# Gathering the next expert's rows in two fp32r passes from a high and a low part

## What is computed

```python
logits = hf @ router_w                       # hf: 256 x 1024, 8 experts
top_vals, top_idx = lax.top_k(logits, 2)
top_w = jax.nn.softmax(top_vals, axis=-1)    # gates: 256 x 8, two entries of each row
for e in range(8):
    y = y + gates[:, e:e+1] * ((silu(hf @ wg[e]) * (hf @ wu[e])) @ wd[e])
```

## Time and profile before

| | |
|---|---|
| median of 3 runs | 1638.24 us (1637.22 to 1639.24) |
| profiled execution, its own time | 1640.91 us |
| its span, first to last instruction | 1639.2 us |
| mean granted TensorE clock | 0.967 |
| PE busy | 1547.0 us, 94% |
| PE weight loads busy | 1292.2 us, 79% |
| DVE busy | 1238.8 us, 76% |
| ScalarE busy | 915.4 us, 56% |
| GpSimd busy | 25.3 us, 2% |
| expert loop | from 814.3 us to about 1620 us |

### The profile page before, as it was taken

One profiled execution on the slowest core, in us unless ns is written; L12 is line 12 of the kernel. 1 busy time (PEld: TensorE's weight loads), 2 busy tenths in 40 slices (PEclk: granted clock), 3 DMA queues, 4 the chain that ended last, 5 costly groups with the idle time before them and its releaser, 6 DMA issues.

```text
span 1639.2 us, 23240 instructions
## 1 busy us (share of the span) xinstructions
PE 1547.0 (94%) x8684; PEld 1292.2 (79%) x8684; DVE 1238.8 (76%) x1408; ACT 915.4 (56%) x952; POOL 25.3 (2%) x60
## 2 busy tenths in 40 slices
PE   5899999899998999989599999999999999999996
PEld 4788777798997887777488888888888888888885
DVE  5969676474356587765688887988879888798886
ACT  5144553433233434543467776767777677676764
POOL 0000010000000000100000000000000000000000
PEclk9699999899899999999699999999999999999999
DMA  5253325444345253324288898988989889899893
GB/s 227 92 162 134 111 85 191 156 173 155 111 157 204 88 189 149 129 97 173 94 337 347 325 376 329 355 336 324 366 312 365 348 324 363 323 357 355 320 365 150
DMA packets 76638, 391.49 MB, mean 239 GB/s; under 512 B 28320, under 2 KB 28448, under 8 KB 29728
## 3 DMA queue, kind: packets, MB, share of 16 engines
q1 hardware_dynamic: 74960, 389.71, 63.2%
q10 hardware_dynamic: 1616, 0.92, 0.2%
HBM read 386.80 MB, written 1.05 MB: 237 GB/s over the span
## 4 chain that ended last, share of the span: by engine, by line
PE 86%; DVE 7%; ACT 4%; issue 2%; DMA 1%; POOL 0%; DVEq 0%; ACTq 0%; POOLq 0%; SPq 0%
PE psum L1609 25%; PE psum L1610 25%; PE psum L1611 25%; PE psum L1625 3%; PE psum L1666 2%; ACT w_hi L524 2%; DVE w_lo L530 2%; PE psum L1649 1%; PE psum L1876 1%; PE psum L1643 1%; DVE hsT_lo L1165 1%; PE psum L1668 1%; ACT prob L892 1%; PE psum L1708 1%; PE psum L1892 0%
## 5 line engine op out<-in xcount | busy, mean ns | idle before, releaser
L530 DVE TENSOR_TENSOR w_lo<-w_raw,w_hi 128x2048 fp32r<-128x2048 f32 x270 | 614.3, 2288 | 213.2 <-ACT w_hi L524 210.4
L524 ACT ACTIVATE w_hi<-w_raw 128x2048 fp32r<-128x2048 f32 x270 | 513.5, 1911 | 313.1 <-PE psum L1611 281.2
L1609 PE MATMUL psum<-w_hi,hsT_hi 128*128 128x512 f32 (+1 forms) x512 | 190.3, 372 | 6.4 <-issue 6.4
L1610 PE MATMUL psum<-w_hi,hsT_lo 128*128 128x512 f32 (+1 forms) x512 | 189.4, 370 | 0.0
L1611 PE MATMUL psum<-w_lo,hsT_hi 128*128 128x512 f32 (+1 forms) x512 | 188.1, 367 | 0.0
L1609 PE MATMUL psum<-w_hi,hT_hi 128*128 128x512 f32 x384 | 156.6, 408 | 2.7 <-DVE w_lo L530 1.2
L1611 PE MATMUL psum<-w_lo,hT_hi 128*128 128x512 f32 x384 | 151.7, 395 | 0.0
L1610 PE MATMUL psum<-w_hi,hT_lo 128*128 128x512 f32 x384 | 151.6, 395 | 0.0
L530 DVE TENSOR_TENSOR w_lo_more<-w_raw,w_hi_more 128x2048 fp32r<-128x2048 f32 x56 | 128.0, 2285 | 21.5 <-ACT w_hi_more L524 21.5
L1609 PE MATMUL psum<-hT_hi,w_hi 128*128 128x256 f32 x416 | 119.9, 288 | 0.8 <-DVE act_ff L1388 0.8
L1610 PE MATMUL psum<-hT_hi,w_lo 128*128 128x256 f32 x416 | 119.1, 286 | 0.0
(11 more groups left out here) (365 smaller groups left out, 2843.8 us busy)
## 6 DMA issues: line engine op xcount, KB each, us to landing
w_raw<-in_stream SPq DMA_DIRECT2D x326, 1024.0 KB, 5.2
w_raw_more<-in_stream SPq DMA_DIRECT2D x40, 1024.0 KB, 6.7
x_tok<-in_x SPq DMA_DIRECT2D x1, 1024.0 KB, 5.0
uT_lags<-uT_by_lag SPq DMA_DIRECT2D x64, 16.0 KB, 1.9
zT_by_lag<-uT_lags SPq DMA_DIRECT2D x64, 16.0 KB, 1.9
out_trunk<-out_tok SPq DMA_DIRECT2D x2, 512.0 KB, 2.7
s_direct<-s_direct_lags SPq DMA_DIRECT2D x40, 16.0 KB, 2.1
s_b_raw<-in_s_b SPq DMA_DIRECT2D x2, 256.0 KB, 6.1
```

The lines of the kernel that those rows point to most:

```text
L524: nc.scalar.activation(split_of(seg, i)[0], raw_of(seg, i), ACT.Copy).then_inc(s_hi, 1)
L530: nc.vector.tensor_tensor(l_, raw_of(seg, i), h.bitcast(F32), ALU.subtract).then_inc(s_lo, 1)
L1609: mm(out, lh, rh, start=start, stop=False)
L1610: mm(out, ll, rh, start=False, stop=False)
```

## The change

Two new tiles hold a high and a low part of the normalised input. `x_normed_hi` lies where `hT_lo` was and is written by ScalarE behind the router's matmuls (two copies of 128 x 1024 to fp32r, ahead of the Exp of `gate_den`). `x_normed_lo` lies over `xn` itself and is written by GpSimd (two subtractions of 128 x 1024) once the gather for the first round, which still reads `xn` as plain fp32, is done. `select` becomes an fp32r tile. The gather for the next round, inside the loop, has for each chunk and token tile two fp32r matmuls in place of one plain fp32 matmul. The transposes of `select` read it as fp32, as before. PE waits for the low part ahead of the gather of half 0.

```diff
-        S = at("select", [P, NT, P], F32, a_att)
+        S = at("select", [P, NT, P], F32R, a_att)
+        xnh = at("x_normed_hi", [P, NT, D], F32R, a_hT + 8192)
+        xnl = at("x_normed_lo", [P, NT, D], F32R, a_v)
@@ GpSimd, behind the constants of the routing stage
+            pool.wait_ge(s_xh, NT)
+            pool.wait_ge(s_tr, TR_AT[1, "hs", 1] + 1)
+            for q in range(NT):
+                nc.gpsimd.tensor_tensor(xnl[:, q, :], xn[:, q, :], xnh[:, q, :].bitcast(F32), ALU.subtract).then_inc(s_xl, 1)
@@ ScalarE, ahead of the Exp of gate_den
+            act.wait_ge(s_tr, TR_AT[1, "logitsT", 0] + 1)
+            for q in range(NT):
+                nc.scalar.activation(xnh[:, q, :], xn[:, q, :], ACT.Copy).then_inc(s_xh, 1)
@@ PE; the old gather stays as gather_whole for the first round
+            def gather(b, g):
+
+                for kk in range(4):
+                    k = 4 * g + kk
+                    for q in range(NT):
+                        mm(b[:, kk * P:(kk + 1) * P], xnh[:, q, k * P:(k + 1) * P], S[:, q, :],
+                           start=(kk == 0 and q == 0), stop=False)
+                        i = mm(b[:, kk * P:(kk + 1) * P], xnl[:, q, k * P:(k + 1) * P], S[:, q, :],
+                               start=False, stop=(kk == 3 and q == 1))
+                i.then_inc(s_tr, 1)
@@ PE, in the loop
                     if i == 30:
                         pe.wait_ge(s_S, r + 2)
+                        pe.wait_ge(s_xl, NT)
                         gather(tr_bank_r(r, "hs0"), 0)
```

## The result

| | before | changed |
|---|---|---|
| median, 14 runs each | 1638.92 us (1637.22 to 1641.88) | 1642.74 us (1640.54 to 1646.19) |
| ratio | 1 | 1.0022, 95% interval 1.0015 to 1.003 |
| profiled execution: span | 1639.2 us | 1639.8 us |
| mean granted TensorE clock | 0.967 | 0.969 |
| GpSimd busy | 25.3 us | 30.0 us |

The changed kernel takes 0.22% longer, 3.6 us by the ratio. The two profiled spans differ by less. That is no contradiction: in the changed kernel's profiled execution the last step ahead of any changed instruction, DVE's copy of the router's logits, comes at 793.24 where it came at 796.18 before, in code that the change doesn't touch. So single executions are read stage by stage.

What follows compares the result with a forecast made beforehand. TensorE (PE) was taken to bound the expert loop, busy 99.64 of 100 us. PE 0, `select` +0.13, ScalarE 0 and GpSimd on DVE +3.4 gave +3.5 on 1638.24, so 1641.8 us; range 1635 to 1645.

Steps and rivals of the forecast that it cites:

- PE's time is unchanged because the load sets the pace: Loop's gather: 16 fp32r matmuls 0.112 us apart, set by weight loads, so a half stays 1.79 us; taken as 0.
- The first half's time is covered, only the second counts: Loop's gather: PE waits 0.19 us behind the first half, so only 8 second halves count, -0.6 to +1.1 us.
- rival (b): Gather: load hidden, only streaming counts, 0.065 us a matmul; second halves 0.75 us shorter, 6.0 us gained, 1635.7; chance 0.05.
- `select` in fp32r, +0.13 us: DVE's `select` pair ahead of the loop: writing fp32r costs between 0 and 0.24 us, taken as +0.13.
- ScalarE's copies cost nothing: Routing stage: two high-part copies on idle ScalarE move the Exp some 0.1 us, covered; cost 0.
- GpSimd holds DVE's chain, +3.4 us: Routing stage: two subtractions of 1.9 us from 807.95 hold `over_prod` and later DVE work; +3.4, bounds 0 to +4.5.
- Rival (a): Gather: fp32r with few moving columns runs at a whole fp32 matmul's pace, 0.223 us; 27 us more, 1668.9; chance 0.19.
- Rival (c): Routing stage and gather: GpSimd and PE cost nothing, 1638.4; within the forecast's own case (0.76), no separate chance.

Runs made afterwards that it cites:

- half_loads: The changed kernel with 64 instead of 128 stationary columns in every matmul of the new gather; 1639.59 us, ratio 1.0003 to the kernel before.
- bf16_two: The changed kernel with the loop's gather from two bf16 parts, `select` read as bf16, subtractions put off into the loop; 1636.12 us, ratio 0.9983 to the kernel before.
- first_short: The changed kernel with the low part's matmuls left out of the gather's first half only; 1642.84 us, ratio 1.0023 to the kernel before.
- second_short: The changed kernel with the low part's matmuls left out of the gather's second half only; 1639.31 us, ratio 1.0001 to the kernel before.
- plain: The changed kernel with the loop's gather as plain fp32 again, reading the high part alone; 1641.45 us, ratio 1.0016 to the kernel before.
- late: The changed kernel with one more wait, so GpSimd's two subtractions start only after round 0's first scatter was taken; 1639.56 us, ratio 1.0002 to the kernel before.
- memsets: The changed kernel with GpSimd's two subtractions replaced by five memsets of a 128 x 1024 tile; 1639.61 us, ratio 1.0007 to the kernel before.
- bf16_three: The changed kernel with the loop's gather from three bf16 parts, 24 matmuls a half, GpSimd making two parts in round 0; 1642.66 us, ratio 1.0025 to the kernel before.

## Why the prediction was right

It forecast 1641.8 us (+3.5) against a measured +3.6 (ratio 1.0022), with the new gather at nothing and the loss in DVE's routing chain, where it was put. That the two numbers agree to 0.1 us is partly luck: two errors in the GpSimd term cancel, as told below. Point by point:

- **PE's time is unchanged because the load sets the pace.** Right. Forecast 0.112 us, measured 0.1115, and half_loads and bf16_two show that it is the load: lighter loads under the same columns give 0.061 and 0.057.
- **The first half's time is covered, only the second counts.** Right, by first_short (nothing gained) and second_short. The term itself was 0 here, so it wasn't tested by the change, only by the experiments. They show that the step was too generous for a gain: part of the second half's saving goes into another wait for eactT_lo, 0.3 us long. Even 0.9 us saved there gave 3.5 us in 8 rounds, so rival (b)'s 0.75 would have given no more than about that, not 6.0.
- **`select` in fp32r, +0.13 us.** Wrong, it is free: the pair takes 0.48 us as before, and one instruction 0.28.
- **ScalarE's copies cost nothing.** Right. From the logits to the start of the Exp it was 2.02 us and is 2.02; the copies end at 795.24, the Exp starts at 795.26.
- **GpSimd holds DVE's chain, +3.4 us.** Right in cause and sum, 3.7 measured in the chain, but not in its detail. The forecast had GpSimd start with ScalarE and hold `over_prod`. It started 0.48 us later, when `over_prod` was nearly through, and held the copies behind it, which have one input. In plain's execution `over_prod` started 0.32 us behind ScalarE's hsT_hi, not 0.16, and was held as forecast (2.57 us). And an instruction took 2.34 us, not 1.9. The two errors have opposite signs: with two subtractions of 2.34 from 805.04 on, the same reckoning gives some 4.3. The price is two holds, of whatever instruction DVE has next, and rows of both kinds had been found. The estimate worked out from the Trainium skill, GPSIMD Engine Reference, section Elementwise — side-by-side cycle accounting (half of its 4497 ns, so 2.25 us), was nearer to the measured 2.34 than the prediction's 1.9.
- **Rival (a)**, the pace of a whole fp32 matmul, fell: 0.1115 against 0.223. **Rival (b)** fell with the loads. The Trainium skill's FP8 and Floating Point Precision, section TensorE Precision Notes, counts four passes for true FP32. The trace agrees as far as streaming goes: in the kernel before, the plain fp32 product of kT and qT holds PE for 0.63 us with 256 moving columns (155.54 to 156.17) and for 0.42 with 128 (156.33 to 156.75), so 1.6 ns a column where fp32r has 0.43. But passes aren't time where the load is as long as the streaming.
- **Rival (c)**, GpSimd for nothing, fell with late.

What stays open: a price of the new gather below some 1.8 us, and why the cast of `rounds` in memsets wasn't held while the one ahead of it was.

## What to carry to other kernels

Before matmuls are split into cheaper passes, look at the pace of the loads: with a fresh stationary tile for every 128 moving columns, the two 32-bit loads of a plain fp32 matmul (0.223 us) took as long as all of its streaming (0.21 us by the 1.6 ns a column above). Two fp32r matmuls load twice as well, so halving the streaming gave nothing, and only a lighter load did (bf16, or 64 columns). An idle GpSimd is not free: ask what DVE does in the same microseconds, and put long GpSimd instructions apart and where DVE has slack; one added wait was worth 3.3 us here (ratios 1.0022 and 1.0002). And a microsecond saved on the busiest engine counts only where no wait follows it: 0.9 us saved in either half of the same gather was worth 0 and about 0.45 us a round.

## What the runs showed of the hardware

- fp32r with 128 moving columns and 128 stationary ones: 0.1115 us a matmul; with 64 stationary ones 0.061; bf16 with 128 and 128: 0.057. All at a granted clock of 1.00, the 2.4 GHz level.
- A GpSimd subtraction of 128 x 1024 floats takes 2.34 us, a memset of the same tile 0.95. The subtraction started 0.48 us after ScalarE, which waits for the same matmul (memsets: 0.44).
- A DVE copy of 128 x 3 floats that met a GpSimd subtraction lasted until that had ended: 1.91 us instead of 0.17. `over_prod` (two inputs) did so in plain: 2.57 us for three instead of 0.42. The DVE reduction ahead of the copy ran beside the subtraction at its old 0.28 us, and hsT_lo, with PSUM as one input, beside a memset at its old 2.16 (memsets); it met no subtraction in the routing stage.
- After 4.0 us without a matmul (bf16_three) the granted clock was 0.50 from 845 to 850, and fp32r matmuls with 512 columns started 0.43 us apart instead of 0.23.
